# Splitting each weight chunk into high and low part by halves of 1024 columns

## The chip, the cores and the metric

The kernel runs on one core of one Trainium2 chip. The metric is the device time of one execution in microseconds (us); smaller is better.

## The reference

The program is two transformer-like blocks, each of two layers, on one sequence of 256 tokens with 1024 features, all in float32. What matters here is that both are long rows of dense products with large weights, with a smaller mixer between them:

```python
def first_block(x, ...):            # 2 layers
    z = rms_norm(x) @ w_in + b_in    # 1024 -> 5640 columns, then attention and an mLSTM
    x = x + (ga * (ya @ w_proj_att) + gb * (yb @ w_proj_mlstm)) @ w_out
    x = x + square(relu(rms_norm(x) @ w_ff1)) @ w_ff2

def second_block(x, ...):           # 2 layers
    x = x + 0.5 * rmsnorm(swiglu_ffn(rmsnorm(x), w_gu, w_down))
    z = rmsnorm(x) @ w_in            # four branches: gmlp, pooling, top-k sparse attention, 31-tap conv
    y = sum(gates[n] * (branch[n] @ w_branch[n]) for n in range(4))
    x = x + rmsnorm(y @ w_out)
    x = x + 0.5 * rmsnorm(swiglu_ffn(rmsnorm(x), w_gu, w_down))
```

Every float32 product with weights is made of three passes on TensorE: the weight is split into a high part (the weight rounded to the matmul's own format) and a low part (the weight less its high part), the activations likewise, and high times high, high times low and low times high are summed.

## The kernel before

The weights come as 326 chunks of 128 x 2048 values (1 MB each): 63 chunks per layer of the first block, then 99 per layer of the second, then two that are loaded and split ahead and never used. Three slots hold them. One slot of `raw` takes the load, one of `w_hi` the high part, one of `w_lo` the low part.

A chunk c goes through four engines in this order.

- SyncE (SP) loads chunk c into `raw` when `lo_ready` says that the low part of chunk c - 3 is made (lines 463 to 471, 1354 to 1361).
- ScalarE (ACT) makes the high part, `split_high`, line 152: one activation Copy over 2048 columns. It waits for the load and, through `chunk_done`, for TensorE to be done with chunk c - 3.
- VectorE (DVE) makes the low part, `split_low`, line 159: one `tensor_tensor` subtract over 2048 columns, `raw` less `w_hi`, both in SBUF. It waits for `hi_ready`.
- TensorE (PE) waits for `lo_ready` of the chunk and runs its matmuls (`product`, lines 183 to 185, called from `f_chunk`, `t_chunk` and `t_last`).

ACT and DVE have other work: they evict PSUM, apply nonlinearities, norms, the top-k search and half of the convolution. Each engine executes its queue in order, and the place of every `split_high` and `split_low` in that queue is written by hand: `high.upto(c)` and `low.upto(c)` issue the splits up to chunk c at that point of the program. ACT is to be some two chunks ahead of PE, DVE one. So whatever stands behind a split in a queue waits for it, and a split waits for what stands ahead of it.

The stretch to which the prediction comes back is the mixing stage of the second block. Its chunks are called M0 + i there. Between M0 + 10 and M0 + 18 the DVE queue holds, in turn, splits, eight rounds of a top-8 search (`MAX8`, `MATCH_REPLACE8`, lines 1682 and 1687), the masks and maxima of the softmax (1699 to 1710), and 15 taps of the convolution (line 1639, two `scalar_tensor_tensor` of 256 columns each). In the same time GpSimd (POOL) makes the other 16 taps: for each, two scalings of 256 columns (line 1293) and one addition of 512 columns (line 1303), each waiting for the one before. Then come four chunks BR + 0 to 3 for the branches, and four chunks WO + 0 to 3 of `w_out`. For each BR chunk DVE multiplies four gates into PSUM results (line 1785), POOL adds the four (two additions at line 1333, the sum at line 1335), ACT makes the high part of the sum (line 1512), and DVE the low part (line 1774, `mix_low`). DVE's queue there reads: split BR + i + 1, four L1785, `mix_low` of the one before; `low.upto(BR + 5)`, the last `mix_low`, then the splits of WO + 2 and WO + 3.

At each norm, DVE scales its rows (line 261), makes one low part of a chunk, and then the low parts of the normed activations (line 304), while PE transposes (line 282).

Of the kernel before, what the change touches and what calls it, by code (L numbers as in the profile page):

```python
# [8 lines left out]
F32, F32R, I32 = mybir.dt.float32, mybir.dt.float32r, mybir.dt.int32  # L9
ACT = mybir.ActivationFunctionType  # L10
# [6 lines left out]
CH = 2048  # L17
# [129 lines left out]
def split_high(k, act, st, layer, c, trips=0):  # L147

    s = c % SLOTS
    act.wait_ge(k.raw_loaded[s], st.loads(layer, c, trips))  # L150
    act.wait_ge(k.chunk_done, st.count(layer, c, trips))
    act.activation(k.w_hi[:, s, :], k.raw[:, s, :], ACT.Copy).then_inc(k.hi_ready, 1)  # L152


def split_low(k, dve, st, layer, c, trips=0):

    s = c % SLOTS
    dve.wait_ge(k.hi_ready, st.count(layer, c, trips))
    dve.tensor_tensor(k.w_lo[:, s, :], k.raw[:, s, :], k.w_hi[:, s, :].bitcast(F32),  # L159
                      ALU.subtract).then_inc(k.lo_ready, 1)  # L160


def split_ahead(split, k, eng, st, layer, n):
# [165 lines left out]
def first_block(nc, k, d, sems):  # L329

    with ExitStack() as ctx:
# [142 lines left out]
        def _(act):  # L474
# [5 lines left out]
            for b in range(2):  # L480
                ins = act.activation(line[:, 2 * b:2 * b + 2, 0:SEQ], k.ps[:, b, :].rearrange("p (h n) -> p h n", h=2), ACT.Copy)
            ins.then_inc(line_ready.sem, 1)
            split_ahead(split_high, k, act, st, 0, AHEAD_HIGH)
            with act.Fori(0, DEPTH) as l:
                high = Splitter(split_high, k, act, st, l, AHEAD_HIGH)
                norm_stats(k, act, l, 0)
                norm_scale(k, act, l, 0)
# [115 lines left out]
                def unit(j, c_up, highs, trips=0, q=0):  # L603

                    act.wait_ge(k.chunk_done, st.results(l, c_up, trips))
                    if j >= 3:
                        act.wait_ge(hid_ready.sem, l * FF_A + q + (j - 2))
                    act.activation(hid_r[:, j % 3, :], k.ps[:, j % 3, :], ACT.Relu).then_inc(relu_ready.sem, 1)
                    if highs:
                        split_high(k, act, st, l, highs[0], trips)  # L610
                    act.wait_ge(sq_ready.sem, l * FF_A + q + (j + 1))
                    act.activation(hidH[:, j % 3, :], hid_r[:, j % 3, :], ACT.Copy).then_inc(hidH_ready.sem, 1)
                    for c in highs[1:]:
                        split_high(k, act, st, l, c, trips)
# [12 lines left out]
        def _(dve):  # L627
# [34 lines left out]
            dve.wait_ge(k.x_loaded, 16 * TT)  # L662
            dve.sem_inc(k.x_new.sem, TT)
            split_ahead(split_low, k, dve, st, 0, AHEAD_LOW)

            with dve.Fori(0, DEPTH) as l:
                low = Splitter(split_low, k, dve, st, l, AHEAD_LOW)
                ch = Chain(dve_chain.sem, DVE_A)

# [223 lines left out]
                def unit(j, lows, trips=0, q=0):  # L893

                    dve.wait_ge(relu_ready.sem, l * FF_A + q + (j + 1))
                    r = hid_r[:, j % 3, :]
                    dve.tensor_tensor(r, r, r, ALU.mult).then_inc(sq_ready.sem, 1)
                    if lows:
                        split_low(k, dve, st, l, lows[0], trips)
                    dve.wait_ge(hidH_ready.sem, l * FF_A + q + (j + 1))  # L900
                    dve.tensor_tensor(hidL[:, j % 3, :], r, hidH[:, j % 3, :].bitcast(F32), ALU.subtract)\
                        .then_inc(hid_ready.sem, 1)
                    for c in lows[1:]:
                        split_low(k, dve, st, l, c, trips)
# [1278 lines left out]
```

## Time and profile before

| what | value |
|---|---|
| runs | 2154.41, 2158.28, 2161.58 us, median 2158.28 |
| profiled execution, first to last instruction | 2153.0 us |
| PE busy | 1982.4 us, 92% of the span |
| DVE busy | 1243.6 us, 58% |
| ACT busy | 923.8 us, 43% |
| POOL busy | 240.0 us, 11% |
| granted TensorE clock, mean | 0.964 |

The profile shows no time of its own for the profiled execution beside its span; the span lies 5.3 us under the median of the runs. "L159" is line 159 of the kernel. A row of the timeline gives start and duration in us, engine, line, operation, what is written and read, its shape, and a count when neighbours of one kind are merged; in brackets stands how long the engine had been idle before it and what it waited for.

### The profile page before, as it was taken

What the parts mean: (1) busy time and instruction counts of PE and PEld (TensorE: products, weight loads), DVE (VectorE), ACT (ScalarE), POOL (GpSimd) and SP (SyncE); (2) the same over time, 40 slices, a digit from 0 to 9 for tenths busy, and PEclk for the clock granted to TensorE, in tenths of its full rate; (3) what the DMA queues carried; (4) which work ended last, traced back from release to release, by engine and by line L of the source; (5) the groups of instructions that cost most, each with busy time, mean ns of one, the idle gap of its engine ahead of it and who ended that gap; (6) DMA issues with size and microseconds to landing.
All of it is one profiled execution on the core that took longest, in us unless ns stands there. A gap on an engine that the chain in (4) does not pass through costs nothing.

```text
span 2153.0 us, 34518 instructions
## 1 busy us (share of the span) xinstructions
PE 1982.4 (92%) x13728; PEld 1856.8 (86%) x13728; DVE 1243.6 (58%) x1465; ACT 923.8 (43%) x943; POOL 240.0 (11%) x181
## 2 busy tenths in 40 slices
PE   6989899998998997999799988997999799988996
PEld 5989899888998996999699878996999699978996
DVE  5675655558565555444559565445444559565544
ACT  4444444435435444343434434434443434434342
POOL 0000000000000001000057140000000047240000
PEclk9999999999999998999899999998999999999998
DMA  6434455444354554555334445554555334344553
GB/s 253 176 131 144 158 195 181 171 157 154 118 189 159 190 184 156 177 194 178 125 138 158 158 155 176 184 186 146 179 180 190 127 137 157 140 174 163 189 186 116
DMA packets 50658, 356.83 MB, mean 166 GB/s; under 512 B 5968, under 2 KB 6128, under 8 KB 8432
## 3 DMA queue, kind: packets, MB, share of 16 engines
q1 hardware_dynamic: 47904, 344.06, 45.4%
q0 software_dynamic: 2640, 11.18, 1.6%
q8 instruction: 80, 1.31, 0.2%
q14 instruction: 34, 0.28, 0.0%
HBM read 353.12 MB, written 2.10 MB: 165 GB/s over the span
## 4 chain that ended last, share of the span: by engine, by line
PE 41%; issue 9%; DVE 6%; POOL 3%; ACT 1%; DVEq 0%; POOLq 0%; ACTq 0%
PE ps L183 13%; PE ps L184 13%; PE ps L185 13%; DVE w_lo L159 1%; DVE conv_y L1639 1%; POOL RL L1333 1%; PE ps L282 1%; DVE pss L129 1%; POOL GU L1335 1%; POOL GU L1333 1%; DVE b_gates L1567 1%; DVE score L1687 0%; DVE top L1682 0%; POOL RL L1335 0%; POOL sum L1311 0%
## 5 line engine op out<-in xcount | busy, mean ns | idle before, releaser
L159 DVE TENSOR_TENSOR w_lo<-raw,w_hi 128x2048 fp32r<-128x2048 f32 x325 | 756.9, 2332 | 512.8 <-ACT w_hi L152 512.3
L183 PE MATMUL ps<-aH,w_hi 128*128 128x256 f32 x3088 | 888.0, 288 | 19.1 <-DVE w_lo L159 12.8
L184 PE MATMUL ps<-aL,w_hi 128*128 128x256 f32 x3088 | 881.8, 286 | 0.0
L185 PE MATMUL ps<-aH,w_lo 128*128 128x256 f32 x3088 | 881.0, 285 | 0.0
L152 ACT ACTIVATE w_hi<-raw 128x2048 fp32r<-128x2048 f32 x326 | 622.9, 1912 | 473.2 <-PE ps L185 471.8
L183 PEld LDWEIGHTS ps<-aH,w_hi 128*128 128x128 f32 x3088 | 600.9, 195 | 26.2 <-issue 18.9
L184 PEld LDWEIGHTS ps<-aL,w_hi 128*128 128x128 f32 x3088 | 600.9, 195 | 2.4
L185 PEld LDWEIGHTS ps<-aH,w_lo 128*128 128x128 f32 x3088 | 600.2, 194 | 0.0
L183 PE MATMUL ps<-w_hi,mixH 128*128 128x512 f32 x608 | 237.6, 391 | 0.0
L184 PE MATMUL ps<-w_lo,mixH 128*128 128x512 f32 x608 | 237.6, 391 | 0.0
L185 PE MATMUL ps<-w_hi,mixL 128*128 128x512 f32 x608 | 236.7, 389 | 0.0
L185 PEld LDWEIGHTS ps<-w_hi,mixL 128*128 128x128 f32 x608 | 114.3, 188 | 24.1
L183 PEld LDWEIGHTS ps<-w_hi,mixH 128*128 128x128 f32 x608 | 114.5, 188 | 21.9
L184 PEld LDWEIGHTS ps<-w_lo,mixH 128*128 128x128 f32 x608 | 114.5, 188 | 21.1
L183 PE MATMUL ps<-w_hi,aH 128*128 128x512 f32 (+1 forms) x320 | 123.3, 385 | 6.1 <-DVE w_lo L159 4.7
L184 PE MATMUL ps<-w_lo,aH 128*128 128x512 f32 (+1 forms) x320 | 122.0, 381 | 0.0
L185 PE MATMUL ps<-w_hi,aL 128*128 128x512 f32 (+1 forms) x320 | 121.8, 381 | 0.0
L1375 ACT ACTIVATE GU<-ps 128x512 f32<-128x512 f32 x44 | 26.3, 597 | 161.7 <-PE ps L185 161.7
L282 PE MATMUL ps<-consts,b_gates 128*128 128x128 f32 x96 | 21.8, 422 | 72.9 <-ACT b_gates L270 72.9
L282 PEld LDWEIGHTS ps<-consts,b_gates 128*128 128x128 f32 x96 | 19.6, 226 | 75.4 <-ACT b_gates L270 75.4
L183 PEld LDWEIGHTS ps<-w_hi,aH 128*128 128x128 f32 x320 | 60.7, 190 | 20.6 <-issue 6.7
L183 PE MATMUL ps<-mixH,w_hi 128*128 128x256 f32 x256 | 73.1, 286 | 5.4 <-DVE w_lo L159 2.2
(321 smaller groups left out, 1723.9 us busy)
## 6 DMA issues: line engine op xcount, KB each, us to landing
raw<-in_w_b SPq DMA_DIRECT2D x200, 1024.0 KB, 4.8
raw<-in_w_a SPq DMA_DIRECT2D x126, 1024.0 KB, 4.8
rows<-in_post_gains POOLq DMA_DIRECT2D x7, 512.0 KB, 4.1
rows<-in_rows_a POOLq DMA_DIRECT2D x2, 1028.0 KB, 6.6
rows<-in_par_b POOLq DMA_DIRECT2D x3, 385.0 KB, 3.5
x<-in_x SPq DMA_DIRECT2D x2, 512.0 KB, 4.2
bias_line<-a_gates POOLq DMA_DIRECT2D x1, 1024.0 KB, 13.1
out<-x SPq DMA_DIRECT2D x2, 512.0 KB, 3.6
```

Source lines behind the costliest of these rows:

```text
L129: dve.scalar_tensor_tensor(t[:, c], y[:, c], y[:, c], v[:, c], ALU.mult, ALU.mult).then_inc(ch.sem, ch.one())
L152: act.activation(k.w_hi[:, s, :], k.raw[:, s, :], ACT.Copy).then_inc(k.hi_ready, 1)
L159: dve.tensor_tensor(k.w_lo[:, s, :], k.raw[:, s, :], k.w_hi[:, s, :].bitcast(F32), ALU.subtract).then_inc(k.lo_ready, 1)
L183: pe.matmul(out, a[0], b[0], start=first, stop=False)
L184: pe.matmul(out, a[0], b[1], start=False, stop=False)
L185: return pe.matmul(out, a[1], b[0], start=False, stop=end)
L282: ins = pe.transpose(k.ps[:, 4 + b, kk * SEQ + tt * P:kk * SEQ + (tt + 1) * P], k.xs[:, tt, kt * P:(kt + 1) * P], k.ident)
L1333: pool.tensor_tensor(g[n], g[n], g[n + 1], ALU.add).then_inc(ch.sem, ch.one())
L1335: pool.tensor_tensor(g[0], g[0], g[2], ALU.add).then_inc(mix_ready.sem, 1)
L1375: act.activation(hid_r[:, j % 2, :], k.ps[:, 2 * (j % 2), :], ACT.Silu).then_inc(silu_ready.sem, 1)
L1567: ins = dve.scalar_tensor_tensor(k.xs[:, tt, :].rearrange("p (b n) -> p b n", b=2), k.ps[:, 4 + 2 * tt:6 + 2 * tt, :], r, gain_row[:, :].r ...
L1639: ins = dve.scalar_tensor_tensor(conv_y[:, f, :], src, w, conv_y[:, f, :], ALU.mult, ALU.add)
```

## The change

Both splits are made by halves of 1024 columns. ACT issues two activations for a chunk and raises `hi_ready` after each, so that the semaphore counts halves. DVE issues two subtracts, each behind a wait for its own half. `lo_ready` is raised once, after the second subtract. The loads, `chunk_done` and what TensorE does are as before.

```diff
@@ split_high @@
-    act.activation(k.w_hi[:, s, :], k.raw[:, s, :], ACT.Copy).then_inc(k.hi_ready, 1)
+    for h in range(2):
+        cols = slice(h * CH // 2, (h + 1) * CH // 2)
+        act.activation(k.w_hi[:, s, cols], k.raw[:, s, cols], ACT.Copy).then_inc(k.hi_ready, 1)
@@ split_low @@
-    dve.wait_ge(k.hi_ready, st.count(layer, c, trips))
-    dve.tensor_tensor(k.w_lo[:, s, :], k.raw[:, s, :], k.w_hi[:, s, :].bitcast(F32),
-                      ALU.subtract).then_inc(k.lo_ready, 1)
+    for h in range(2):
+        cols = slice(h * CH // 2, (h + 1) * CH // 2)
+        dve.wait_ge(k.hi_ready, st.count(layer, c, trips) * 2 - (1 - h))
+        ins = dve.tensor_tensor(k.w_lo[:, s, cols], k.raw[:, s, cols], k.w_hi[:, s, cols].bitcast(F32), ALU.subtract)
+    ins.then_inc(k.lo_ready, 1)
```

## Rows read from the trace of the kernel before

**Rows 1.** Waits, whole span: engine line waited for, us in total, times, longest
```profile
DVE w_lo L159 <- ACT w_hi L152: 512.3, 225, 11.0
...
PE ps L282 <- ACT b_gates L270: 72.9, 6, 14.7
...
PE ps L183 <- DVE w_lo L159: 19.7, 14, 3.1
PE ps L995 <- DVE hn L791: 10.2, 2, 5.1
```

**Rows 2.** Groups by line: count | busy us, mean ns | idle before, releaser
```profile
L159 DVE TENSOR_TENSOR w_lo<-raw,w_hi 128x2048 fp32r<-128x2048 f32 x325 | 756.9, 2332 | 512.8 <-ACT w_hi L152 512.3
...
L152 ACT ACTIVATE w_hi<-raw 128x2048 fp32r<-128x2048 f32 x326 | 622.9, 1912 | 473.2 <-PE ps L185 471.8 <-DMA raw<-in_w_a 1.3
```

**Rows 3.** Timeline of PE, mixing stage of the second block, first layer
```profile
1162.61 0.38 PE L183 MATMUL ps<-aH,w_hi 128*128 128x256 f32 x1
...
1171.76 0.58 PE L183 MATMUL ps<-aH,w_hi 128*128 128x256 f32 x1 [3.13 <-DVE w_lo L159]
...
1230.72 0.38 PE L183 MATMUL ps<-aH,w_hi 128*128 128x256 f32 x1 [2.26 <-DVE w_lo L159]
...
1268.92 0.49 PE L183 MATMUL ps<-w_hi,aH 128*128 128x512 f32 x1 [0.69 <-DVE w_lo L159]
1275.86 0.49 PE L183 MATMUL ps<-w_hi,aH 128*128 128x512 f32 x1 [1.20 <-DVE w_lo L159]
```

**Rows 4.** Timeline of DVE and ACT where each begins with no wait
```profile
151.60 1.22 DVE L834 TENSOR_TENSOR hn<-hn,small 128x1024 f32<-128x1024 f32 x1
152.74 2.28 DVE L159 TENSOR_TENSOR w_lo<-raw,w_hi 128x2048 fp32r<-128x2048 f32 x1
154.94 0.69 DVE L837 TENSOR_SCALAR mo<-mo 128x1024 f32<-128x1024 f32 x1
...
104.86 1.06 ACT L510 ACTIVATE ya<-mqk 128x1024 f32<-128x1024 f32 x1 [3.10 <-DVE mqk L728]
105.82 1.90 ACT L152 ACTIVATE w_hi<-raw 128x2048 fp32r<-128x2048 f32 x1
...
173.74 1.91 ACT L152 ACTIVATE w_hi<-raw 128x2048 fp32r<-128x2048 f32 x1
175.54 1.05 ACT L585 ACTIVATE mixH<-hn 128x1024 fp32r<-128x1024 f32 x1
```

**Rows 5.** Timeline of DVE, then POOL, while the branches are mixed
```profile
1258.24 0.81 DVE L1774 SCALAR_TENSOR_TENSOR aL<-GU,aH 128x512 fp32r<-128x512 f32 x1
1258.97 3.39 DVE L159 TENSOR_TENSOR w_lo<-raw,w_hi 128x2048 fp32r<-128x2048 f32 x1
...
1249.50 1.30 POOL L1335 TENSOR_TENSOR RL<-RL 128x512 f32<-128x512 f32 x1
...
1258.44 1.77 POOL L1333 TENSOR_TENSOR RL<-RL,y 128x512 f32<-128x512 f32 x1
1260.29 3.22 POOL L1335 TENSOR_TENSOR RL<-RL 128x512 f32<-128x512 f32 x1
```

**Rows 6.** Timeline of DVE, then POOL: two subtracts in direct succession
```profile
1108.39 3.16 DVE L159 TENSOR_TENSOR w_lo<-raw,w_hi 128x2048 fp32r<-128x2048 f32 x1
...
1111.47 2.28 DVE L159 TENSOR_TENSOR w_lo<-raw,w_hi 128x2048 fp32r<-128x2048 f32 x1
...
1109.57 4.89 POOL L1293 TENSOR_SCALAR pooled<-conv_x,rows 128x256 f32<-128x256 f32 x1 [0.17 <-POOL sum L1303]
```

**Rows 7.** Timeline of DVE, mixing stage, before and in the taps
```profile
1116.07 2.70 DVE L159 TENSOR_TENSOR w_lo<-raw,w_hi 128x2048 fp32r<-128x2048 f32 x1 [1.11 <-ACT w_hi L152]
...
...
1162.40 5.95 DVE L1639 SCALAR_TENSOR_TENSOR conv_y<-conv_x,rows,conv_y 128x256 f32<-128x256 f32 x8
1168.27 3.36 DVE L159 TENSOR_TENSOR w_lo<-raw,w_hi 128x2048 fp32r<-128x2048 f32 x1
1171.55 3.24 DVE L1639 SCALAR_TENSOR_TENSOR conv_y<-conv_x,rows,conv_y 128x256 f32<-128x256 f32 x8
```

## The prediction

> **What bounds the kernel now.** I read four views, in this order. The busy times (the table above): PE is busy 1982 of 2153 us, so at most 171 us can be won off its idle time, and the change leaves its matmuls alone. The waits: DVE stands idle 512.3 us, in 225 places, for the high part of a chunk, and that is the wait that the change cuts; but PE waits for a low part only 19.7 us, in 14 places, and waits most for the norms, 72.9 us in six places [rows 1]. So in 225 - 14 places or more a late low part is late for nobody. Then the timeline of PE, to find the 14: all lie in the mixing stage of the second block, seven in each of its two layers, nearly alike in both; four of the first layer's and the start of the chunk ahead of the first are shown [rows 3]. Last the timelines of DVE and POOL around them, to see what made each low part late. In most it is not the high part. DVE is busy without a pause: with splits, search and taps ahead of 1171.76, with gates and splits from 1252 to 1269. What is to be seen in rows 5 and 7 is that a subtract of 2.28 us takes 3.36 to 3.39 us there [rows 5, 6, 7], and a POOL addition of 1.30 us takes 3.22 [rows 5]: the two engines take turns on their operands in SBUF.
>
> **What the change saves.** Where DVE waits for ACT, the chain of a chunk was 1.91 + 2.28 = 4.19 us [rows 2, 6]. By halves it is 1.05 for the first activation, 1.13 until the second subtract begins, 1.22 for it: 3.40, so 0.80 less [rows 4]. Times 225 it is some 180 us of DVE's idle time. What hides it: a high part starts when PE leaves chunk c - 3 [rows 2], so PE has two whole chunks, some 12 us by the 6.0 us between 1162.61 and 1171.76 - 3.13 [rows 3], for a chain of 4.2. The `raw` slot comes free 0.8 us earlier too, and the load starts so much earlier; ACT waited for loads 1.3 us in the whole run [rows 2]. I take 0 for all this. It would count where a late low part has waited for its high part; in the stretches of the 14 the only such wait that I find is 1.11 us at 1116.07, and there a POOL addition follows within the new gap [rows 7]. Bounds: 0 to -0.8 us a layer; I take 0.
>
> **What it adds on ACT and DVE.** An instruction's duration is not what it costs in a queue, since the next begins before it ends. DVE: 1024 columns take 1.14 us from start to start (151.60 to 152.74), 2048 take 2.20 (152.74 to 154.94); two halves cost 2.27, so +0.07 a chunk at most, taken 0.06. ACT: 0.96 (104.86 to 105.82) against 1.80 (173.74 to 175.54), so +0.11 [rows 4]. 326 chunks make 20 us on DVE and 36 us on ACT, which are 58% and 43% busy, and PE does not see them except in these places:
> - The wait of 2.26 us at 1230.72, and one more a layer, have one high part and one low part in their chain: 0.11 + 0.06 = 0.17 each, 0.35 a layer, 0.7 us in all [rows 3].
> - First block: PE waits twice 5.1 us for a DVE chain behind two subtracts [rows 1]: 0.12 each, 0.25 in all. Four norms in which PE waits for `aL` behind one subtract: 0.06 each, 0.25 in all.
> The second wait and the register that holds its value run in DVE's sequencer beside a subtract of 1.1 us; 0 is taken, and at worst the gap of 0.1 us by the durations' overlap is lost at each half.
> The Trainium skill (VectorE: DVE Perf Modes, the section on the TRN2 errata) says that each instruction from SBUF pays a fixed extra, (N + 151) cycles at 0.96 GHz. The durations agree (1.22 and 2.28 us), and by them two halves would cost 0.16 us more than the whole; the starts show 0.06. By 0.16 the sum below would be some 2 us higher.
>
> **What it adds between the halves.** This is the term that decides. A new boundary in the middle of a subtract is a place at which a waiting POOL operation can go first. For it: at 1258.97 a subtract follows `aL` with no pause, an addition of POOL had been waiting since 1258.44, it went first (1.77 us instead of 1.30), and the subtract took 3.39 instead of 2.28, +1.1 [rows 5]. In the taps, where the same meets every boundary, eight instructions take 5.95 us with POOL and 3.24 without [rows 7]. Against it: at 1111.47 one subtract follows another, a POOL scaling had been waiting since 1109.57, and it had to wait for both (4.89 us), while the second subtract took its plain 2.28 [rows 6]. The bounds of one boundary with an addition waiting are 0 and +1.1 us. I take +1.1: what waits in the places that count is mostly an addition, and I find no addition that waited at a boundary and was passed over. For a scaling, which holds DVE up much less, 0.2.
> The Trainium skill (SBUF — State Buffer, "SBUF: two separate sides") says that VectorE instructions with two SBUF inputs and GpSimd instructions share one pair of ports, held by whichever starts first for its whole instruction. Rows 5 agree to the tenth of a us (3.39 - 2.28 = 1.1). It would give the +1.1; that a waiting GpSimd operation can be passed over, as in rows 6, it doesn't say.
>
> Branch mixing. Three subtracts stand in series from 1252 to 1269, with gates between and no pause of DVE; the second is shown. An addition (L1335, 3.22 us) waits behind each [rows 5]. Each gets 1.1 + 0.06 = 1.16: the chunk that PE began at 1268.92 comes 3.5 later, at 1272.4. It runs 1275.86 - 1.20 - 1268.92 = 5.74 us, to 1278.2, and the next one's low part is made by then (its wait of 1.20 goes), so PE begins at 1278.2 instead of 1275.86 [rows 3]: +2.3 a layer, **4.6 us**. Bounds +0.2 and +3.5 a layer.
>
> Search and taps. Between 1127 and 1168 stand six subtracts. Walking DVE and POOL through the rows, three of the new boundaries meet an addition and three a scaling: 3 x 1.1 + 3 x 0.2 + 6 x 0.06 = 4.3 us late. But POOL's work is fixed, and what it does earlier it doesn't do later: the tap group of 5.95 falls to 3.24 and the subtract of 3.36 to 2.28, 3.8 back [rows 7], so the low part for 1171.76 is only 0.5 late. The chunk ahead of it was begun as soon as its low part was ready (1162.61) and is now 4.6 late; it takes PE 6.0, to 1173.2. PE begins the chunk of 1171.76 at 1173.2 [rows 3]: +1.5 a layer, **3.0 us**. Bounds: 0, and 4.6 a layer if nothing is given back.
>
> **The sum.** 4.6 + 3.0 + 0.7 + 0.25 + 0.25 = 8.8 us. The profiled span goes from 2153.0 to 2161.8; with the 5.3 us by which it lies under the median of the runs, the forecast is **2167 us**, +0.4%. Its own range, by the bounds in which POOL does enter: 2162 to 2174.
>
> **The rivals.**
> *POOL doesn't enter between halves* (rows 6 hold for additions too). Then only the 0.06 remain: 0.2 in the mixing and 0.4 in the taps a layer, 1.2 in all, and 1.2 for the small terms: 2160.7, no change that can be measured. For it: rows 6 are the nearest in kind, two subtracts of one line. Against: rows 5 and 7. It decides if the subtracts ahead of 1171.76 and in the branch mixing keep POOL's sum at 3.2 us.
> *Faster.* POOL enters, but mostly with scalings or beside the search, whose operations have one input and don't stop for it. Then DVE gets back the 3.8 us of rows 7 and the first wait's 0.8 and pays 6 x 0.26 = 1.6 us: it is 3.0 ahead at 1171.76, and the wait of 3.13 goes, in both layers -6.2 us [rows 3]: 2152. It decides if at most one of the six boundaries meets an addition, and the branch mixing doesn't pay. Against it: in the mixing nothing but additions waits.
> *The change doesn't do what it says*: the second subtract finds its half not ready, or the sequencer adds 0.1 us at each half. ACT's half of 0.96 is shorter than DVE's 1.13, so the first is out; the second would show as slower on all subtracts, +2 us on top.
>
> **How the numbers follow.** 0.3% is 6.5 us, about what a measurement of this kernel can tell from no change. Forecast 0.50, of which four fifths lie above 2164.8; POOL kept out 0.37; faster 0.10, half of it beyond 0.3%, with a little for a saving that I don't see; slower by something else 0.03. So slower 0.43, same 0.48, faster 0.09. The range for 8 in 10 leaves out the better part of the faster case and the top of the forecast's: 2154 to 2173.
>
> **What the changed profile would show.** DVE's wait for the high part falls from 512 us by some 180, PE's waits for a low part don't fall with it. Subtracts of 1.22 us, of which some twelve to twenty in the mixing stage take 2.3, one of the two halves of a chunk and sometimes both. POOL's sum (3.22) falls to 2.1 or so in the forecast; if it stays at 3.2 POOL was kept out. POOL's taps end some us sooner against the search. The start of the chunk at 1268.92 moves against that at 1230.72 by 3.5 us. What would make it wrong: that an addition is passed over between halves; that POOL's earlier additions fall beside the search more than I walked; or a part of the idle 171 us that follows another chain than I read.

## The result and the profile after

The changed kernel takes 2166.7 us (median of 7 executions, 2163.8 to 2167.4), the kernel before 2158.5 us in the same session (7 executions, 2154.4 to 2161.6). The ratio is 1.0037 with a 95% interval of 1.0026 to 1.0048: 8 us slower. The forecast was 2167.0. The total came out as forecast; its parts did not, and most of what follows is about that. The profiled execution is one of those timed, and not the median one. The changed kernel took 2165.4 us in it. The kernel before took, by its span of 2153.0 us, most likely the 2154.4 us of its fastest: in all other profiles the time is 1.6 to 2.1 us above the span.

The page of the changed kernel, its busy line and the two split groups (against [rows 2]; line numbers are 2 to 4 higher than before):

```profile
span 2163.7 us, 35239 instructions
PE 1990.1 (92%) x13728; PEld 1864.1 (86%) x13728; DVE 1274.6 (59%) x1790; ACT 954.5 (44%) x1269; POOL 230.7 (11%) x181
...
L163 DVE TENSOR_TENSOR w_lo<-raw,w_hi 128x1024 fp32r<-128x1024 f32 x650 | 793.1, 1263 | 417.2 <-ACT w_hi L154 416.2
...
L154 ACT ACTIVATE w_hi<-raw 128x1024 fp32r<-128x1024 f32 x652 | 653.0, 1052 | 463.7 <-PE ps L189 462.3
```

The first thing to read is PE's own line. The span is 10.7 us longer (2153.0 to 2163.7), with the same 13728 matmuls. PE's idle time, span less busy, went from 2153.0 - 1982.4 = 170.6 to 2163.7 - 1990.1 = 173.6: only 3.0 us. The other 7.7 us are busy time: the same matmuls took longer, and the mean granted clock went from 0.964 to 0.958. Not all of this is owed to the change, as the experiment before_again shows.

The waits of the changed kernel, against [rows 1]:

```profile
DVE w_lo L163 <- ACT w_hi L154: 416.2, 207, 10.8
...
PE ps L286 <- ACT b_gates L274: 72.9, 6, 14.7
...
PE ps L187 <- DVE w_lo L163: 22.4, 15, 2.4
```

DVE's wait fell by 96 us, and PE's waits for a low part rose by 2.7. Where PE waits in the mixing stage of the first layer is in its timeline, against [rows 3]:

```profile
1165.03 0.38 PE L187 MATMUL ps<-aH,w_hi 128*128 128x256 f32 x1 [0.75 <-ACT b_gates L1458]
1172.99 0.47 PE L187 MATMUL ps<-aH,w_hi 128*128 128x256 f32 x1 [1.95 <-DVE w_lo L163]
...
1214.77 1.16 PE L1893 MATMUL ps<-consts,y 128*128 128x128 f32 x8 [0.64 <-DVE consts L1753]
1217.11 0.38 PE L187 MATMUL ps<-aH,w_hi 128*128 128x256 f32 x1 [1.19 <-DVE w_lo L163]
1234.01 0.38 PE L187 MATMUL ps<-aH,w_hi 128*128 128x256 f32 x1 [2.42 <-DVE w_lo L163]
...
1254.37 0.38 PE L187 MATMUL ps<-mixH,w_hi 128*128 128x256 f32 x1 [0.40 <-DVE w_lo L163]
1261.96 0.38 PE L187 MATMUL ps<-mixH,w_hi 128*128 128x256 f32 x1 [1.58 <-DVE w_lo L163]
1269.55 0.49 PE L187 MATMUL ps<-w_hi,aH 128*128 128x512 f32 x1 [1.58 <-DVE w_lo L163]
1277.12 0.49 PE L187 MATMUL ps<-w_hi,aH 128*128 128x512 f32 x1 [1.83 <-DVE w_lo L163]
```

The start at 1217.11 is that of chunk M0 + 22, the one at 1234.01 that of M0 + 24. Two places matter. The last four rows are the branch mixing: 0.40 + 1.58 + 1.58 + 1.83 = 5.4 us of waits. The kernel before has four there too. Two are in [rows 3], and the two ahead of them are these:

```profile
1256.06 0.38 PE L183 MATMUL ps<-mixH,w_hi 128*128 128x256 f32 x1 [1.11 <-DVE w_lo L159]
...
1262.49 0.49 PE L183 MATMUL ps<-w_hi,aH 128*128 128x512 f32 x1 [0.43 <-DVE w_lo L159]
```

With the 0.69 and 1.20 of [rows 3] that is 3.4 us. The other place is between 1217.11 and 1234.01. From the one start to the other are 16.9 us; less the wait at the end, 16.90 - 2.42 = 14.5. Before, the same matmuls took 15.22 - 2.26 = 13.0 (from 1215.50 to 1230.72). No wait explains these 1.5 us. A table by windows does. Its columns: window and length in us; busy us (and instructions) of PE, PEld, DVE, ACT and POOL; granted clock; DMA share and GB/s. First the changed kernel, both layers, then the same places before.

```profile
1217.50:1220.90 3.40, 3.40 (x18) 3.40 (x18) 2.65 (x3) 0.69 (x2) 0.00 (x0) 0.50 0.84 272
1234.60:1238.00 3.40, 3.40 (x19) 3.40 (x18) 3.40 (x4) 0.00 (x0) 0.00 (x0) 0.50 0.68 270
1869.40:1872.80 3.40, 3.40 (x18) 3.40 (x18) 2.65 (x3) 0.68 (x2) 0.00 (x0) 0.51 0.73 279
1886.50:1889.90 3.40, 3.40 (x18) 3.40 (x18) 3.40 (x4) 0.00 (x0) 0.00 (x0) 0.50 0.85 289
```

```profile
1215.50:1218.90 3.40, 3.40 (x28) 3.40 (x29) 2.03 (x2) 1.31 (x3) 0.00 (x0) 1.00 0.64 214
1230.70:1234.10 3.40, 3.38 (x28) 3.38 (x29) 3.40 (x2) 0.34 (x1) 0.00 (x0) 1.00 0.63 198
1864.20:1867.60 3.40, 3.40 (x28) 3.40 (x29) 2.08 (x2) 1.26 (x3) 0.00 (x0) 1.00 0.65 243
1879.40:1882.80 3.40, 3.40 (x28) 3.40 (x29) 3.40 (x2) 0.29 (x1) 0.00 (x0) 1.00 0.67 214
```

PE shows as busy nearly throughout in all eight, but does 18 or 19 matmuls in the stretch after and 28 before. Right behind the waits that grew from 1.12 to 1.19 and from 2.26 to 2.42 the clock is at 0.5, the lower of its two levels (1.2 against 2.4 GHz), for 3.4 us. Four such stretches at 1.5 us each are 6 of the 7.7 us. The rest is a sum of differences of up to 2 us in other places, of both signs.

In the branch mixing DVE and POOL read so, against [rows 5]:

```profile
1257.29 4.54 DVE L163 TENSOR_TENSOR w_lo<-raw,w_hi 128x1024 fp32r<-128x1024 f32 x2
...
1264.88 4.53 DVE L163 TENSOR_TENSOR w_lo<-raw,w_hi 128x1024 fp32r<-128x1024 f32 x2
```

```profile
1256.78 1.74 POOL L1337 TENSOR_TENSOR GU<-GU,yb 128x512 f32<-128x512 f32 x1
1258.61 2.15 POOL L1339 TENSOR_TENSOR GU<-GU 128x512 f32<-128x512 f32 x1
```

A pair of halves takes 4.5 us where a whole subtract took 3.4, and POOL's sum 2.15 instead of 3.22. The first half waits for POOL's second addition as before; the second half now waits for the sum, which gets in at the new boundary. Each half takes 2.3 us instead of 1.2. From pair to pair are 7.59 us, against PE's 5.74 for a chunk. The Trainium skill (SBUF — State Buffer, "SBUF: two separate sides") says that the shared ports belong to whichever instruction starts first, for its whole length. These rows agree within 0.2 us: the second addition ended at 1256.78 + 1.74 = 1258.52, 1.2 us after the first half began, and each half was held by 1.1 us.

### The profile page after: what moved, and what is told of

It reads as the page before. It is cut to its first block, busy times and chain, and to the rows that moved or that the text cites. A ratio compares the mean times of both kernels' runs of the same rounds, so it can differ in the third digit from the quotient of the medians.

```text
span 2163.7 us, 35239 instructions
## 1 busy us (share of the span) xinstructions
PE 1990.1 (92%) x13728; PEld 1864.1 (86%) x13728; DVE 1274.6 (59%) x1790; ACT 954.5 (44%) x1269; POOL 230.7 (11%) x181
## 4 chain that ended last, share of the span: by engine, by line
PE 48%; DVE 8%; issue 3%; ACT 1%; DVEq 0%; POOL 0%; ACTq 0%; POOLq 0%
PE ps L187 16%; PE ps L188 16%; PE ps L189 16%; DVE w_lo L163 2%; PE ps L286 1%; DVE pss L129 1%; DVE b_gates L1571 1%; ACT w_hi L154 0%; DVE GU L1789 0%; DVE RL L1789 0%; DVE x L1580 0%; DVE conv_y L1643 0%; PE ps L1942 0%; DVE pss L135 0%; DVE tmp L129 0%
## 5 line engine op out<-in xcount | busy, mean ns | idle before, releaser
L163 DVE TENSOR_TENSOR w_lo<-raw,w_hi 128x1024 fp32r<-128x1024 f32 x650 | 793.1, 1263 | 417.2 <-ACT w_hi L154 416.2
L154 ACT ACTIVATE w_hi<-raw 128x1024 fp32r<-128x1024 f32 x652 | 653.0, 1052 | 463.7 <-PE ps L189 462.3
L1379 ACT ACTIVATE GU<-ps 128x512 f32<-128x512 f32 x44 | 26.3, 597 | 159.5 <-PE ps L189 159.5
```

Of the source, the lines that this page charges most:

```text
L154: act.activation(k.w_hi[:, s, cols], k.raw[:, s, cols], ACT.Copy).then_inc(k.hi_ready, 1)
L163: ins = dve.tensor_tensor(k.w_lo[:, s, cols], k.raw[:, s, cols], k.w_hi[:, s, cols].bitcast(F32), ALU.subtract)
L1379: act.activation(hid_r[:, j % 2, :], k.ps[:, 2 * (j % 2), :], ACT.Silu).then_inc(silu_ready.sem, 1)
```

## The experiments

All ratios are to the kernel before in the same session. PE idle is span less PE busy, of the one profiled execution; the clock is that execution's too. It was the slowest of its kernel's executions in act_only and late_as_halves and 3.5 us above the median in order_whole, and the fastest in feat_halves, so that PE busy of two kernels can be compared only roughly.

| kernel | median us | ratio (95%) | PE idle | PE busy | clock |
|---|---|---|---|---|---|
| changed kernel | 2166.7 | 1.0037 (1.0026 to 1.0048) | 173.6 | 1990.1 | 0.958 |
| before_again | 2157.4 | 1.0001 (0.9992 to 1.0011) | 169.8 | 1985.3 | 0.962 |
| act_only | 2163.0 | 1.0022 (1.0013 to 1.0031) | 173.9 | 1989.6 | 0.959 |
| dve_only | 2163.1 | 1.0026 (1.0017 to 1.0035) | 172.9 | 1986.5 | 0.960 |
| whole_in_mixing | 2163.0 | 1.0022 (1.0013 to 1.0031) | 169.7 | 1989.2 | 0.960 |
| late_by_one | 2159.2 | 1.0010 (1.0000 to 1.0020) | 170.9 | 1984.0 | 0.964 |
| feat_halves | 2150.1 | 0.9969 (0.9958 to 0.9980) | 167.8 | 1979.1 | 0.964 |
| pool_short_whole | 2142.8 | 0.9932 (0.9918 to 0.9947) | 159.5 | 1981.8 | 0.963 |
| pool_short_halves | 2149.8 | 0.9962 (0.9947 to 0.9977) | 161.4 | 1987.5 | 0.960 |
| late_as_halves | 2161.1 | 1.0011 (1.0000 to 1.0021) | 170.9 | 1991.6 | 0.959 |
| feat_whole | 2149.3 | 0.9958 (0.9944 to 0.9972) | 165.1 | 1982.0 | 0.964 |
| order_whole | 2140.2 | 0.9915 (0.9901 to 0.9930) | 157.4 | 1984.6 | 0.961 |
| order_halves | 2150.4 | 0.9963 (0.9950 to 0.9975) | 163.5 | 1985.3 | 0.960 |

**The kernel before once more.** No edit.

> The kernel before once more, to see how much the granted clock moves between executions of one kernel. In the two profiles TensorE (PE) is idle 170.6 us before and 173.6 after, and busy 1982.4 and 1990.1, while the mean granted clock is 0.964 and 0.958. So 3.0 us of the 10.7 are idle time and 7.7 are matmuls that ran at the lower clock. If the clock's share belongs to the change, this run shows a clock of 0.961 or more and 2158 us. If it is scatter of one execution, its profile may show 0.958 at the same program, and PE busy 1988 or more.

It shows 0.962 and 1985.3 us, so about 3 of the 7.7 us of busy time lie within what one program does. One wait of 1.12 us at 152.88 in the profile before is absent in this one and in the changed kernel's alike, and both are busy 1.8 and 1.7 us longer between 120 and 240 us. Against before_again the changed kernel has 3.8 us more idle time and 4.8 us more busy time. The 79 executions of the kernel before in these sessions whose clock was recorded tell more: 18 at a mean clock of 0.964 took 2155.3 us on average, 24 at 0.962 took 2157.2, 10 at 0.960 took 2161.0. So the time of this one program moves by some 6 us along with its clock. The changed kernel had 0.958 to 0.960 in all of its 7 executions, the kernel before in 15 of 79. At equal clock (0.960, 0.959, 0.958) the changed kernel took 2163.8, 2166.7 and 2166.3 us and the one before 2161.0, 2162.2 and 2160.9: 3 to 5.5 us, of few executions and of different sessions. The rest of the 8 us goes with the lower clock, which the changed kernel has nearly always.

**One engine's halves alone.** In act_only the activation is cut and the subtract is not; in dve_only the other way round.

```diff
 act_only @@ split_low @@
+    dve.wait_ge(k.hi_ready, st.count(layer, c, trips) * 2)
+    dve.tensor_tensor(k.w_lo[:, s, :], k.raw[:, s, :], k.w_hi[:, s, :].bitcast(F32), ALU.subtract)
```

> Only ScalarE's activation is cut into halves; VectorE makes its subtract whole and waits for both halves. First theory (a waiting POOL addition goes between DVE's halves): nothing of the loss, 2158 to 2160 us, branch mixing idle as before (PE waits of 1.11, 0.43, 0.69 and 1.20 us there), DVE's wait for the high part up by 0.11 us a chunk. Rival (ACT's extra 0.11 us a chunk, or any shift of the times, moves the clock's low stretches): 2163 us or more with the mixing's waits unchanged.

> Only VectorE's subtract is cut into halves, each behind the same wait for the whole high part. First theory: all of the loss, 2165 to 2167 us, both subtracts of 1024 columns taking 2.3 us in the branch mixing, four waits there of 5.4 us in sum a layer instead of 3.4. Rival: 2159 to 2161, because the cost hangs on ACT's half.

Neither came out as the first theory had it. ScalarE's halves alone cost as much as VectorE's, 5 us, and no POOL operation goes anywhere because of them: the mixing's waits are 1.11, 0.43, 0.72 and 1.20, as before within 0.03. For act_only that is the rival's outcome in the times (2163.0 against its 2163 or more). In it the waits grow a little (2.26 becomes 2.35 at M0 + 24; 0.39 becomes 0.50 at the eight small matmuls just ahead of M0 + 22), and a stretch of 3.4 us at half clock follows the 2.35 in both layers. Its idle time of 173.9 holds 2.1 us of one norm at 1510.14, where PE waited 15.07 us instead of 12.99; no other profile shows that, and it stays unexplained. In dve_only the mixing's four waits are the 5.4 us expected (0.40, 1.58, 1.58, 1.84), and the total was 2 us less than expected.

**The branch mixing alone.** The changed kernel with whole subtracts for the four low parts a layer that are made while the branches are mixed.

```diff
+    parts = 1 if st.base and 60 <= c <= 63 else 2
+    for h in range(parts):
...
```

> The changed kernel, but the four low parts a layer that are made while the branches are mixed are whole. First theory: PE's waits in the mixing return to 3.4 us a layer, 3.9 us less idle in both layers, and 2160 to 2163 us are left, by what the halves cost in other places and at the lower clock. If the search and taps carried a loss of 3.0 as my forecast had it, 2162 or more. Rival (a boundary between halves costs nothing here): 2166 to 2167, no difference to the changed kernel.

The waits are back:

```profile
1258.70 0.38 PE L188 MATMUL ps<-mixH,w_hi 128*128 128x256 f32 x1 [1.11 <-DVE w_lo L164]
1265.14 0.49 PE L188 MATMUL ps<-w_hi,aH 128*128 128x512 f32 x1 [0.43 <-DVE w_lo L164]
1271.58 0.49 PE L188 MATMUL ps<-w_hi,aH 128*128 128x512 f32 x1 [0.72 <-DVE w_lo L164]
1278.65 0.49 PE L188 MATMUL ps<-w_hi,aH 128*128 128x512 f32 x1 [1.34 <-DVE w_lo L164]
```

PE's idle time falls by 3.9 us to 169.7, which is that of the kernel before, and the ratio from 1.0037 to 1.0022, 3 us, though the two intervals just overlap. So POOL's additions between the halves cost what they take in these waits, and with them gone the halves still cost 5 us with no idle time to show for it.

**GpSimd's share.** Both kernels with its taps and branch additions cut to one column each; their sums are left out.

```diff
...
-                    pool.tensor_tensor(g[0], g[0], g[2], ALU.add).then_inc(mix_ready.sem, 1)
+                    pool.tensor_tensor(g[0][:, 0:1], g[0][:, 0:1], g[2][:, 0:1], ALU.add).then_inc(mix_ready.sem, 1)
```

> The kernel before, with GpSimd's taps and branch additions cut to one column each (their sums are left out), so that it hardly touches SBUF beside VectorE. Theory: subtracts of 2.28 us everywhere in the mixing stage, the waits of 3.13 us and of 3.4 us in the branch mixing go in each layer: 2143 to 2147. It is the partner of the next kernel.

> The changed kernel with the same cut of GpSimd's work. First theory: what the halves cost while the branches are mixed (3.9 us, all by GpSimd's additions between them) is gone, and 4 to 5 us are left over its partner, by the small delays on ScalarE and VectorE and the clock that follows them. Rival (the halves' cost in the mixing is their own, whatever GpSimd does): 8 us over the partner.

Without POOL there is no wait in the mixing in either, and halves cost 7.0 us by the medians (0.0030 of the ratio, give or take 0.002), more than the 4 to 5 expected; with that interval the time alone tells neither theory from the rival's 8. The rival's mechanism is ruled out by the profile, since halves bring no wait in the mixing here. Idle time is 1.9 us of it. In the profile all four places have the stretch (clock 0.50 in each), and none in the partner. The parts (7 without POOL, 8 with it, 3 by the mixing) add up only within some 3 us, which is what the intervals leave.

**Making the waits longer without halves.** The kernel before, with small operations ahead of the late low parts, one a layer in late_by_one, four in late_as_halves.

```diff
 late_as_halves
...
+                dve.tensor_scalar(cstat[:, 3, 0:1], cstat[:, 0, 0:1], 1.0, None, ALU.mult)
+                dve.tensor_scalar(cstat[:, 3, 1:2], cstat[:, 0, 1:2], 1.0, None, ALU.mult)
                 low.upto(BR + 1)
```

> The kernel before with one small VectorE operation (0.17 us, its result unused) ahead of the low part for which PE waits 2.26 us at 1230.72, once a layer. In the six profiles so far, a stretch at half clock (0.5, 3.4 us long) began within this wait or just behind it in five of six places with a wait of 2.35 to 2.43 us, in one of two with 2.32, and in none of four with 2.26. Theory (a wait that grows by 0.1 us costs a stretch at half clock): the wait is 2.4 us, the stretch appears in most such places, PE busy rises by 1.5 us for each, and the kernel is 2 to 3.5 us slower, 2158.5 to 2160. Rival (the clock's stretches fall by chance or follow other work): 0.3 us slower, nothing that can be measured.

> The kernel before, no halves anywhere, with four small VectorE operations of 0.17 us or less a layer (results unused) so that two waits of PE become as long as in the changed kernel: one ahead of the inverse root (0.39 becomes 0.6), one ahead of the low part of M0 + 22 (1.12 becomes 1.2), two ahead of that of M0 + 24 (2.26 becomes 2.4 or 2.5). By the ten profiles so far, the place of the 1.12 us shows a stretch at half clock in none of 12 where the two waits are 0.39 to 0.50 and 1.12 to 1.19, and in five of six where they are 0.65 and 1.19; the place of 2.26 in none of six, in three of six with 2.32 to 2.35, in five of six with 2.42. Theory (these stretches are most of what the halves cost): 0.6 us a layer of waits and up to four stretches of 1.5 us, 2160 to 2163, near the 2163.0 of the halves on ScalarE alone. Rival (the stretches come with the halves or by chance): 1.2 us slower, 2158.

One operation made the wait 2.33 us, less than meant, and the profile shows no stretch; its ratio of 1.0010 (1.0000 to 1.0020) would fit either theory. Four operations gave these waits and, in windows behind them, these clocks:

```profile
1216.21 1.16 PE L1893 MATMUL ps<-consts,y 128*128 128x128 f32 x8 [0.47 <-DVE consts L1750]
1218.56 0.43 PE L183 MATMUL ps<-aH,w_hi 128*128 128x256 f32 x1 [1.19 <-DVE w_lo L159]
...
1235.40 0.38 PE L183 MATMUL ps<-aH,w_hi 128*128 128x256 f32 x1 [2.38 <-DVE w_lo L159]
```

```profile
1218.70:1222.10 3.40, 3.40 (x17) 3.40 (x18) 2.31 (x2) 1.03 (x2) 0.00 (x0) 0.51 0.68 229
1235.80:1239.20 3.40, 3.40 (x18) 3.40 (x18) 3.40 (x2) 0.00 (x0) 0.00 (x0) 0.50 0.83 263
```

Layer two shows the same (0.50 and 0.51). So the stretches come without any half. All profiles together, a place counted once for each layer:

| place | waits of PE, us | profiled kernels | at half clock |
|---|---|---|---|
| M0 + 22 | 0.39 to 0.50, then 1.12 | before (2), late_by_one, pool_short_whole, act_only | 0 of 10 |
| M0 + 22 | 0.40, then 1.19 | dve_only | 0 of 2 |
| M0 + 22 | 0.46 to 0.65, then 1.19 | changed, whole_in_mixing, pool_short_halves, late_as_halves | 7 of 8 |
| M0 + 24 | 2.25 to 2.27 | before (2), pool_short_whole | 0 of 6 |
| M0 + 24 | 2.32 to 2.36 | late_by_one, dve_only, act_only | 3 of 6 |
| M0 + 24 | 2.38 to 2.43 | changed, whole_in_mixing, pool_short_halves, late_as_halves | 7 of 8 |

The 7 of 8 are the same seven layers at both places, so the two rows are not two independent proofs; in the eighth, the first layer of whole_in_mixing, neither place has a stretch, though its waits of 0.65, 1.19 and 2.42 us are as long. The length of these waits makes a stretch likely and doesn't settle it.

The clocks of all timed executions point the same way. Of the executions of the four kernels with grown waits, 24 of 34 had a mean clock of 0.960 or less (changed 7 of 7, whole_in_mixing 5 of 11, pool_short_halves 3 of 4, late_as_halves 9 of 12). Of those of the kernel before it was 15 of 79, and 6 of 17 in late_as_halves' own session. act_only had 8 of 11, dve_only 5 of 11 and late_by_one 4 of 12, so the mean clock alone doesn't tell at which place it was lost.

The time itself is weaker evidence: 1.0011, which is 2.4 us with an interval from nothing to 4.5, between the rival's 1.2 and the theory's 4 or more. The kernel before had much of the low clock itself in that session (median 2159.2 against 2156.3 and 2156.7 in the two others). And the profile with all four stretches is that of its slowest execution (2164.2 us; the fastest, at a clock of 0.963, took 2154.8).

**Taking the waits away.** M0 + 22 and M0 + 24 are made earlier, in time in which VectorE stood idle, in both kernels.

```diff
-                low.upto(M0 + 21)
+                low.upto(M0 + 22)
                 dve.wait_ge(css_ready.sem, css_ready.at(l, 2))
...
-                low.upto(M0 + 22)
                 dve.wait_ge(lt_ready.sem, lt_ready.at(l, 1))
...
-                low.upto(M0 + 23)
+                low.upto(M0 + 24)
                 dve.wait_ge(y3H_ready.sem, y3H_ready.at(l, 1))
```

> The changed kernel, with the low parts of M0 + 22 and M0 + 24 moved ahead in VectorE's queue, into idle time that it has there (4.9 us ahead of 1210.3, and from 1219.8 on): M0 + 22 ahead of the wait for the variance, M0 + 24 ahead of the activation split that follows. Both high parts are made in time. Theory: the waits of 1.19 and 2.42 us a layer go, 7.2 us, and with them up to four stretches at half clock of 1.5 us each: 2154 to 2158, that is 9 to 12 us under the changed kernel. Rival (the clock is no matter of these waits): 7.2 under it, 2159.5. Second rival (the next wait grows instead): 2163 or more.

> The kernel before with the same two moves as feat_halves (M0 + 22 and M0 + 24 ahead). Theory: the waits of 1.12 and 2.26 us a layer go, 6.8 us, and no clock comes back with them since there was no stretch at half clock behind them: 2146 to 2150, so that halves cost 0 to 4 us where these waits are gone, against 8 to 9 with them; what is left is the mixing's 3.9. Rival (the halves cost what they cost wherever these waits stand): 2141 to 2142, 8 us under feat_halves.

On the halves the two moves are worth 0.0068 of the ratio, 14.7 us, twice the 7.2 us of waits that they remove and more than the 9 to 12 expected; PE busy falls from 1990.1 to 1979.1, and no execution had a clock under 0.962. On the whole splits they are worth 0.0042, 9 us, as expected. Between the two kernels are now 0.0011, 2.4 us (interval about ±0.0018, each measured against the kernel before in its own session), where they were 0.0037 apart. This is the timed evidence that in this order of the queue most of what halves cost hung on these two waits.

**A better order.** In addition, M0 + 16 to 18 each ahead of four taps, and each low part of the mixing one chunk earlier.

```diff
-                for c in (15, 16, 17):
+                low.upto(M0 + 15)
+                for c in (16, 17, 18):
                     low.upto(M0 + c)
                     conv_taps(4)
-                low.upto(M0 + 18)
...
-                    low.upto(BR + 1 + i)
+                    low.upto(BR + 2 + i)
```

> Whole splits, and every low part for which PE waits in the mixing stage made one place earlier: the two moves of feat_whole, M0 + 16 to 18 each ahead of the four taps that stood before it (their high parts are there 8 us earlier), and BR + 2 ahead of the first four gates, into 8.5 us of VectorE's idle time, with the next ones each one chunk earlier too. Theory: 3.13 us a layer go in the taps, and most of 3.4 us in the branch mixing, since a low part made one chunk ahead starts it with 2.2 us in hand against a deficit of 0.7 a chunk (6.43 by VectorE, 5.74 by PE): 10 to 13 us under feat_whole, 2136 to 2140. Rival (another chain ends at the same time, the convolution's or the loads'): 2143 or more.

> The same order with the splits by halves. Theory: GpSimd's additions still go between the halves, VectorE takes 7.6 us a chunk in the mixing against PE's 5.74, so 1.8 us short a chunk, and the lead of 2.2 us doesn't cover it: 3 us a layer of waits are left there, and it ends 4 to 7 us over order_whole, 2142 to 2146. Rival (with low parts made in time the halves cost nothing): within 2 us of order_whole.

order_whole is the fastest, 0.9915, 18 us under the kernel before and 9 under feat_whole, where 10 to 13 were expected. The one wait for a low part that is left in each layer, and the one that stands in its place with halves (first and second kernel):

```profile
1269.95 0.49 PE L183 MATMUL ps<-w_hi,aH 128*128 128x512 f32 x1 [2.30 <-DVE w_lo L159]
```

```profile
1273.43 0.61 PE L187 MATMUL ps<-w_hi,aH 128*128 128x512 f32 x1 [4.71 <-DVE w_lo L163]
```

Halves cost 0.0048 here, 10 us, more than the 4 to 7 expected: 2.4 us a layer in this wait, 0.56 a layer in another at 1167.02 that the whole splits don't have, 6 us of idle time in all. The other 4 us go with the clock of the timed runs: three of the six executions of order_whole had 0.964 or 0.965 and took 2137.0 to 2138.1 us, none of order_halves was above 0.962. At 0.961 the two took 2143.7 and 2149.4 us, which is the idle time again. In both kernels a stretch at low clock begins in or just behind this wait in each layer, where the kernel before has none; in order_whole so:

```profile
1270.40:1273.80 3.40, 3.40 (x10) 2.62 (x9) 1.62 (x1) 0.00 (x0) 0.00 (x0) 0.50 1.03 434
```

With halves the two last moves bring nothing (0.9963 against the 0.9969 of feat_halves), with whole splits they bring 9 us. The 2.30 us that remain are a low part that stands behind the last `mix_low`, for which VectorE waits 3.2 us; no run has it ahead of that.

## Why the forecast held, and where it didn't

The total of 2167 was hit with a sum of idle time of 8.8 us, of which 3.0 came (3.8 against before_again). The rest came from a cost that the sum doesn't have, the matmuls' own time at the lower clock. That the total fits is luck in part. By its own steps:

- **What it saves.** "Times 225 it is some 180 us of DVE's idle time": this wait fell by 96 us, to 416.2 in 207 places. Most of even that is a change of name. DVE's idle time as a whole went from 2153.0 - 1243.6 = 909.4 to 889.1 us; it is paced by PE, so a chain that is 0.8 us shorter lets it wait elsewhere. That all this is worth 0 to PE was right.
- **What it adds on ACT and DVE.** DVE is 31.0 us more busy and ACT 30.7. The waits grew nearly as priced: 2.26 to 2.42 (0.17 forecast), 1.12 to 1.19 (0.17), 5.12 to 5.23 and 5.24 (0.12); those for `aL` at the norms stayed at 1.5 us in all (0.25 forecast). The 0.39 that became 0.64 wasn't in the sum. The step that failed is that a wait which grows by 0.17 us was priced at 0.17 us. Behind it came a stretch of 3.4 us at half clock, 1.5 us more. Four such stretches are 6 us of the profile's 10.7, and 0.7 was entered for these waits.
- **Between the halves.** That an addition which waits goes first was right in the mixing, for both halves: 4.5 us a pair. POOL's sum came to 2.15 (2.1 forecast). The rival by which POOL is kept out fell. For a scaling 0.2 us was entered; it costs nothing, since in the changed profile all 14 scalings that came up during a first half were passed over. The "agree to the tenth" of rows 5 compares 1.1 with itself: the addition there ended 1.24 us after the subtract had begun.
- **Branch mixing**, 2.3 us a layer forecast, 2.0 measured (5.4 less 3.4), 3.9 in both, and whole_in_mixing gives exactly that back. Mechanism and size were right, the way to it less so: a chunk takes VectorE 7.59 us instead of 6.43 throughout, and PE waits three times for 1.6 to 1.8 us, where I had it catch up after one. The start forecast to move by 3.5 us (1268.92 against 1230.72) moved by 4.9 (1277.12 against 1234.01), which is 3.4 and the 1.5 of the stretch at half clock.
- **Search and taps**, 1.5 us a layer forecast, -0.4 measured: 0.75 + 1.95 against the 3.13 of [rows 3]. This step failed. In the walk three of six boundaries met an addition. In the trace one does, and scalings stand at the others or nothing:

```profile
1142.14 3.16 DVE L163 TENSOR_TENSOR w_lo<-raw,w_hi 128x1024 fp32r<-128x1024 f32 x2
...
1148.18 2.35 DVE L163 TENSOR_TENSOR w_lo<-raw,w_hi 128x1024 fp32r<-128x1024 f32 x2
...
1161.28 3.62 DVE L163 TENSOR_TENSOR w_lo<-raw,w_hi 128x1024 fp32r<-128x1024 f32 x2
```

```profile
1141.78 1.30 POOL L1307 TENSOR_TENSOR sum<-sum 128x512 f32<-128x512 f32 x1
1143.26 3.66 POOL L1297 TENSOR_SCALAR sum<-conv_x,rows 128x256 f32<-128x256 f32 x2 [0.17 <-POOL sum L1307]
...
1148.36 3.78 POOL L1297 TENSOR_SCALAR pooled<-conv_x,rows 128x256 f32<-128x256 f32 x2 [0.17 <-POOL sum L1307]
...
1162.01 1.81 POOL L1307 TENSOR_TENSOR sum<-sum 128x512 f32<-128x512 f32 x1
```

At 1142.14 the first half is held by an addition that had begun before it. The scaling comes at 1143.26, while the first half runs, and the pair ends at 1145.3, 0.8 us later than a plain pair of 2.35 and not 2.2. At 1148.18 a scaling is passed over and the pair is plain. Only at 1161.28 does an addition get in between the halves, and the pair takes 1.3 us more. That is the wait of 0.75 us at 1165.03: this low part ends at 1164.90, and the row names ACT because an eviction of 0.6 us ends 0.02 us after it. In the second layer the same wait (0.56) is put down to the low part, as in dve_only (0.59), and act_only has none. Set against PE's own times, the low part for 1165.03 was thus 0.75 us late instead of the forecast's 4.6. The forecast's 3.8 given back were 1.2 (the tap group took 5.77 instead of 5.95, the subtract 2.35 instead of 3.36), so the next low part came 0.4 us ahead. The *faster* rival's mechanism (scalings at the boundaries) was right for the search and fell with that one addition and the small return. The 4.6 in the prediction's own sum stands without a source beside the 4.3 of its walk.

The search and taps were forecast 3.9 us too high (+3.0 against -0.9 in both layers) and the clock's 6 us were not in the sum; with the small terms these came near to cancelling. The forecast's number is no proof of its reasons. What is shown: the mixing's 3 to 4 us (undone by whole_in_mixing); that half-clock stretches mostly follow the two grown waits, with halves or without (the table of places); that without these waits, in the same order otherwise, halves cost 2.4 us instead of 8. What stays open: how much of the 8 us is owed to the clock in the timed runs, since late_as_halves gave only 2.4 us with a wide interval; why one layer with waits as long has no stretch; why order_halves never reaches the higher clock that order_whole has in half of its executions; and what in ScalarE's halves costs the part of its 5 us beyond two stretches.

## What to carry to other kernels

Read PE's idle and busy time apart before pricing a change: here the same matmuls took 7.7 us more in the profile, and a stretch at half clock of 1.5 us stood behind most waits that had grown by a tenth of a microsecond or two. Profile the unchanged kernel twice, since 3 of these 7.7 us came with no change at all. Shortening a chain that its consumer doesn't wait for brings nothing, and a new instruction boundary on VectorE can let in a GpSimd addition that is already waiting. The gain lay in the order of the queue: look for late operands whose input was ready while the engine that makes them stood idle, and make them there (18 us of 2158, with nothing but lines moved).

## What the runs showed of the hardware

- A stretch at half clock of 3.4 us behind waits of 2.38 us and more in 7 of 8 places, behind 2.25 to 2.27 in none of 6; and behind 1.19 us when 0.46 us or more of idle time stood 2.3 us ahead of it in 7 of 8, behind 1.12 in none of 10. The 7 of 8 are the same seven layers. The Trainium skill (TensorE: Matmul & The Clock Gate, Part 1) ties the clock to how busy TensorE has been recently, and these rows agree.
- One unchanged program took 2154.1 to 2164.3 us, and its mean granted clock, 0.958 to 0.964, goes along with the time.
- Between two subtracts of 1024 columns in direct succession, 12 of the 14 GpSimd additions that came up during the first one went before the second (1162.01 above), and all 14 scalings were passed over (1143.26 and 1148.36 above; between whole subtracts that of [rows 6]). The two additions passed over are one in each layer, that of line 1310 at 1181.62, which took 3.29 us while the pair took its plain 2.34.
